# Scaling a transformer block's mixing products by 1/rms after they are made, with filler matmuls ahead of two norms

## What is computed

```
# end of the first block
x = x + gate2 * rmsnorm(y, g_post_ffn)
# second block, mixing input
h = rms_norm(x, norm_mix_w)          # x * rsqrt(mean(x*x) + eps) * w
proj = h @ w_in                      # 2048 x 5136
q_a, k_a, v_a, q_g, k_g, v_g, r_g, gate_lr = split_cols(proj, IN_SPLITS)
```

## Time and profile before

| | |
|---|---|
| median of 3 runs | 2810.79 us (2810.56 to 2812.27) |
| the profiled execution's own time | 2811.32 us |
| its span, first to last instruction | 2809.6 us |
| PE busy | 2719.9 us (97% of the span) |
| DVE busy | 1805.5 us (64%) |
| ACT busy | 1295.8 us (46%) |
| GpSimd busy | 292.1 us (10%) |
| mean granted clock of PE | 0.986 |

### The profile page before, as it was taken

The page is one execution under the profiler, slowest core; times in us unless marked ns, Lnnn a source line. Parts: engine busy times, 40 slices in busy tenths (PEclk is TensorE's granted clock), DMA queues, the critical chain, the costliest instruction groups (busy, mean ns, idle before and its releaser), DMA issues.

```text
span 2809.6 us, 38901 instructions
## 1 busy us (share of the span) xinstructions
PE 2719.9 (97%) x14799; PEld 2340.4 (83%) x14799; DVE 1805.5 (64%) x2009; ACT 1295.8 (46%) x1556; POOL 292.1 (10%) x161
## 2 busy tenths in 40 slices
PE   4899999999899999999997999999999999999998
PEld 4798888788688888888886989878888888888887
DVE  7966779689965556655576444656666654666655
ACT  2256554334444444444444445535555533555454
POOL 2010121100000100001000000100113210131100
PEclk8899999999999999999998999999999999999999
DMA  9975646698945557755576554545555565555553
GB/s 373 349 261 191 223 150 225 226 325 310 322 140 190 193 198 251 254 180 191 182 254 229 166 171 144 165 139 180 186 189 179 179 209 183 192 180 190 184 197 133
DMA packets 299522, 588.70 MB, mean 210 GB/s; under 512 B 12282, under 2 KB 19438, under 8 KB 298510
## 3 DMA queue, kind: packets, MB, share of 16 engines
q1 hardware_dynamic: 292816, 577.84, 60.5%
q10 hardware_dynamic: 6590, 9.27, 1.0%
HBM read 584.98 MB, written 2.10 MB: 209 GB/s over the span
## 4 chain that ended last, share of the span: by engine, by line
PE 88%; DVE 7%; issue 2%; ACT 1%; DMA 1%; SPq 0%; POOL 0%; DVEq 0%; POOLq 0%; ACTq 0%
PE psum L780 13%; PE psum L784 13%; PE psum L782 13%; PE bank L973 12%; PE psum L973 12%; PE bank L976 6%; PE psum L976 6%; PE psum L791 2%; PE psum L795 2%; PE psum L793 2%; DVE ada_acc L864 2%; DVE mod_acc L651 2%; DVE w_lo L738 2%; PE bank L946 1%; PE bank L2594 1%
## 5 line engine op out<-in xcount | busy, mean ns | idle before, releaser
L738 DVE TENSOR_TENSOR w_lo<-raw,w_hi 128x1024 fp32r<-128x1024 f32 x912 | 1157.0, 1286 | 835.9 <-ACT w_hi L726 826.0
L726 ACT ACTIVATE w_hi<-raw 128x1024 fp32r<-128x1024 f32 x912 | 953.1, 1054 | 1260.9 <-PE psum L784 580.7
L973 PE MATMUL psum<-h_both,w_hi 128*128 128x512 f32 x1408 | 496.5, 397 | 0.8 <-DVE x L2362 0.7
L973 PE MATMUL bank<-h_both,w_hi 128*128 128x512 f32 x1408 | 495.3, 396 | 0.0
L976 PE MATMUL bank<-h_both,w_lo 128*128 128x256 f32 x1408 | 395.0, 281 | 0.0
L976 PE MATMUL psum<-h_both,w_lo 128*128 128x256 f32 x1408 | 394.9, 280 | 0.0
L780 PE MATMUL psum<-w_hi,h_both 128*128 128x512 f32 x880 | 348.4, 396 | 1.3 <-ACT tokbuf L1810 0.7
L784 PE MATMUL psum<-w_hi,h_both 128*128 128x512 f32 x880 | 343.5, 390 | 0.0
L782 PE MATMUL psum<-w_lo,h_both 128*128 128x512 f32 x880 | 343.4, 390 | 0.0
L973 PEld LDWEIGHTS psum<-h_both,w_hi 128*128 128x128 f32 x1408 | 264.2, 188 | 64.1 <-DVE x L2362 1.0
L973 PEld LDWEIGHTS bank<-h_both,w_hi 128*128 128x128 f32 x1408 | 264.1, 188 | 63.3
(11 more groups left out here) (361 smaller groups left out, 3172.8 us busy)
## 6 DMA issues: line engine op xcount, KB each, us to landing
raw<-in_w_in_dram SPq DMA_DIRECT2D x120, 1024.0 KB, 5.1
raw<-in_w_ffn_in_dram SPq DMA_DIRECT2D x88, 1024.0 KB, 5.0
raw<-in_w_ffn_up_dram SPq DMA_DIRECT2D x88, 1024.0 KB, 5.1
raw<-in_w_ada_dram SPq DMA_DIRECT2D x64, 1024.0 KB, 5.2
raw<-in_w_ffn_out_dram SPq DMA_DIRECT2D x44, 1024.0 KB, 5.1
raw<-in_w_ffn_down_dram SPq DMA_DIRECT2D x44, 1024.0 KB, 5.1
ada_raw<-in_w_ada_dram SPq DMA_DIRECT2D x64, 512.0 KB, 8.0
raw<-in_w_out_dram SPq DMA_DIRECT2D x32, 1024.0 KB, 5.2
```

The lines of the kernel that those rows point to most:

```text
L726: nc.scalar.activation(w_hi[:, slot, :, 0:ncol], raw[:, rs, 2 * h:2 * h + 2, 0:ncol], ACT.Copy).then_inc(split_hi, inc)
L738: nc.vector.tensor_tensor(w_lo[:, slot, :, 0:ncol], raw[:, rs, 2 * h:2 * h + 2, 0:ncol], w_hi[:, slot, :, 0:ncol].bitcast(F32), ALU.subtra ...
L973: pe.matmul(region[:, f, :].rearrange("p (s t) -> p s t", s=2), w_hi[:, slot, kk, cols_], h_both[:, :, k, :], start=first, stop=False, ski ...
```

## The change

At norm2 PE transposes x itself, by a transpose with `ident`, as soon as a column block of the residual sum is there, without 1/rms. The products of all groups are therefore made of x times the gain, and 1/rms is applied where a group is taken out of PSUM. For that, DVE takes groups 0 to 3, 6 and 7 out (they need a factor that varies along the free axis, from `r_row`, made by two fp32 matmuls of `ones` by `diag` and a copy), and ACT takes 4, 5 and 9 to 12 out, each in two activations with a scale for each partition. The low-rank gate input moves from ACT to DVE. The order of residual pieces, squares, pairs and weight splits is written out anew on DVE, ACT and PE. ACT issues its four small loads after the norm. `keep_busy` puts 44 matmuls that nobody reads ahead of norm1 and 20 ahead of norm2. In `up2`, ACT and DVE each split one half of the second group's weights before, and not after, their work on the convolution of the first.

```diff
+        ("norm2", (2, 2, 2, 2)), ("r_row", (1, 0, 0, 0))]
...
+        def keep_busy(pe, stage, n):
+
+            pe.wait_ge(bank_free[0], fill(stage, 0))
+            for k in range(n):
+                pe.matmul(bank[:, 0, :].rearrange("p (s t) -> p s t", s=2), h_hi[:, k % KD, 0:P],
+                          h_both[:, :, k % KD, :], start=True, stop=True, skip_group_check=True)
...
# ACT
-            residual_squares_act(act, 3)
+            for c in range(D // COLS):
+                residual_square_act(act, 3, c, 0)
+                for b in (2 * c, 2 * c + 1):
+                    if b > 4:
+                        split_w_hi(act, plan.mix_in2, 0, b - 1, b)
+                    gained_pair_act(act, "norm2", b, gain_of("norm_mix_w_2"))
+                residual_square_act(act, 3, c, 1)
+            split_w_hi(act, plan.mix_in2, 0, 7, 8)
...
-            split_act(act, "norm2", h_hi, KD, gain_of("norm_mix_w_2"), between=plan.mix_in2)
...
-                    if g <= 12 and s == 2:
+                    if g in (4, 5, 9, 10, 11, 12) and s == 2:
...
+                        for t in range(TT):
+                            ins = nc.scalar.activation(dst[:, t, :], ps[:, t, :], kind,
+                                                       scale=stats[:, 4, 2 + t:3 + t])
+                        ins.then_inc(free, 1)
...
# ACT, up2
+                        if g == 0:
+                            split_w_hi(act, ph, i, *span(ph, 1, part=(0, 1)))
...
-                            split_w_hi(act, ph, i, *span(ph, 1, part=(0, 2)))
+                            split_w_hi(act, ph, i, *span(ph, 1, part=(1, 2)))
...
# DVE
             part_sums_dve(dve, 3, part_sq[:, 0])
-            split_w_lo(dve, plan.mix_in2, 0, 3, 4)
             dve.wait_ge(sem("y_gated"), 4)
-            residual_dve(dve, chain, 3)
-            normed_dve(dve, 4)
-            split_dve(dve, "norm2", h_hi, h_lo, KD, gain_of("norm_mix_w_2"), between=plan.mix_in2)
+            dve.wait_ge(sem("rms"), 4)
+            residual_columns_dve(dve, 3, 0)
+            residual_columns_dve(dve, 3, 1)
+            for b in range(KD // 2):
+                if b >= 4:
+                    split_w_lo(dve, plan.mix_in2, 0, b - 1, b)
+                gained_pair_dve(dve, "norm2", b, gain_of("norm_mix_w_2"))
+                if b < 2:
+                    residual_columns_dve(dve, 3, 2 + b)
+            split_w_lo(dve, plan.mix_in2, 0, 7, 8)
+            part_sums_dve(dve, 4, part_sq[:, 1])
...
+                    if at == (0, 0):
+                        split_w_lo(dve, ph, 0, *span(ph, 0, part=(4, 6)))
+                        normed_dve(dve, 4)
+                        split_w_lo(dve, ph, 0, *span(ph, 0, part=(6, 8)))
...
+                    if at == (0, 2):
+                        dve.wait_ge(bank_full[0], filled("r_row", 0))
+                        nc.vector.tensor_copy(r_row[:], bank[:, 0, 0:TOK]).then_inc(bank_free[0], 1)
+                        dve.wait_ge(bank_free[0], emptied("r_row", 0))
...
+                    if g in (0, 1, 2, 3, 6, 7) and s == 2:
+                        dve.wait_ge(w_used, ph.done(0, g))
+                        flat = psum[ph.pair[g]][:].rearrange("p b (f t) -> p (b f) t", t=TOK)
+                        per_token = r_row[:].unsqueeze(1).to_broadcast([P, 4, TOK])
+                        if g < 2:
+                            ins = nc.vector.scalar_tensor_tensor(q2_t[:, 4 * g:4 * g + 4, :], flat, HD ** -0.5,
+                                                                 per_token, ALU.mult, ALU.mult)
+                        else:
+                            dst = k2_t[:, 4 * (g - 2):4 * (g - 1), :] if g < 4 else (qg if g == 6 else kg)[:]
+                            ins = nc.vector.tensor_tensor(dst, flat, per_token, ALU.mult)
...
# PE
+            keep_busy(pe, "norm1", 44)
             pe.wait_ge(sem("normed"), 4)
...
+            ph = plan.mix_in2
+            keep_busy(pe, "norm2", 20)
+            for b in range(4):
+                pe.wait_ge(sem("x_ready"), 8 + 2 * (b // 2 + 1))
+                transpose_pair_pe(pe, "norm2", x, b)
+            for h in range(KD // 2):
+                products(pe, ph, 0, 0, h_hi, h_lo, transposed=True, ready="norm2", part=(h, h + 1))
+                if h < 4:
+                    pe.wait_ge(sem("x_ready"), 8 + 2 * (h // 2 + 3))
+                    transpose_pair_pe(pe, "norm2", x, 4 + h)
             pe.wait_ge(sem("normed"), 6)
-            normed_products(pe, ph, "norm2", 4, transposed=True)
+            pe.wait_ge(bank_free[0], fill("r_row", 0))
+            for t in range(TT):
+                mm = pe.matmul(bank[:, 0, t * P:(t + 1) * P], ones[:], diag[:, t, :], start=t == 0,
+                               stop=t == TT - 1, skip_group_check=True)
+            mm.then_inc(bank_full[0], 1)
```

More of the change, by code:

```diff
@@ L345, in bank_uses @@
         ("up1_1", (FFN_PARTS[1][1],) * 4), ("mod_down1", (0, 0, 0, 2)),
-        ("norm2", (2, 2, 2, 2))]
+        ("norm2", (2, 2, 2, 2)), ("r_row", (1, 0, 0, 0))]
     for at in sorted(SIDE_2):
@@ L419, in build_program @@
         diag = sb("diag", [P, TT, P])
+        r_row = sb("r_row", [P, TOK])
         trig = sb("trig", [P, 2, TT, ROT_HALF])
@@ L1740, in _ @@
                     split_w_hi(act, ph, 0, *span(ph, g, part=part if g else ((4, 8), (8, 8), (8, 8))[s]))
+                    if at == (1, 0):
+                        act.wait_ge(sem("rms"), 5)
+                        act.dma_start(w_up_g[:], a["w_gla_gate_up_2"][0]).then_inc(sem("w_up_g_full"), 16)
                     if at == (10, 0):
@@ L1759, in _ @@
                         nc.scalar.activation(lr_hi[:], raw_lr[:], ACT.Copy).then_inc(sem("lr_hi"), 1)
-                    if at == (4, 1):
-                        act.wait_ge(bank_full[1], filled("low_rank", 1))
-                        nc.scalar.activation(gate_lr[:], bank[0:RANK, 1, 0:TOK], ACT.Copy).then_inc(bank_free[1], 1)
-                    if g <= 12 and s == 2:
+                    if g in (4, 5, 9, 10, 11, 12) and s == 2:
                         act.wait_ge(w_used, ph.done(0, g))
@@ L2326, in up2_dve @@
                     for g in range(2):
-                        split_w_lo(dve, ph, i, *span(ph, g, part=(begun, 8) if g == 0 else None))
+                        split_w_lo(dve, ph, i, *span(ph, g, part=(1 if g else begun, 8)))
                         dve.wait_ge(sem("conv_low"), 2 * (g0 + i) + g + 1)
@@ L2337, in up2_dve @@
                                 dve.sem_inc(bank_free[b], 1)
+                        if g == 0:
+                            split_w_lo(dve, ph, i, *span(ph, 1, part=(0, 1)))
                         dst = (act_g, act_u)[g]
```

48 lines of the change are left out of this document (25 added, 23 removed).

## The result

| | before | after |
|---|---|---|
| median of the runs on the same chip, us | 2811.53 (2810.56 to 2813.80, 4 runs) | 2791.00 (2787.14 to 2796.14, 4 runs) |
| ratio, 95% interval | | 0.9927 (0.9909 to 0.9945) |
| profiled execution: time, span, us | 2811.3, 2809.6 | 2796.14, 2794.4 |
| PE busy | 97% | 98% |
| norm2: last product's start to first transposes, to first product, us | 15.05, 21.05 | 7.10, 10.04 |

The change gains 20.5 us by these medians, where 12.7 was forecast, and its time lies 4.8 us under the range. The forecast's direction holds and its size doesn't. Why it varies is part of the answer.

The account below looks back on a forecast made before the run. PE, busy 97% of the span, was taken as the bound. Norm2's 13.0 less 0.6 for the clock plus 0.3 at norm1 gave 12.7 us off 2811.3, 2798.6; the median 0.5 lower, 2798.1 us; range 2795.8 to 2802.5.

Parts of the forecast that it names:

- the paragraph on up2: In up2, moving one split past the convolution on ACT and DVE: 0, bounded by 1.2 us either way.
- Norm2: At norm2, first products 11.9 us earlier, cheaper transposes 1.5, two fp32 matmuls cost 0.4: gain 13.0 us at full clock.
- the clock term: At norm2, a fall of PE's clock after the pause costs 0 to 1.7 us; 0.6 taken in the sum.
- Pairs 4 to 7: In norm2's group 0, plain transposes cost 0.42 us a pair in place of 0.81: 1.5 us gained.
- rivals 3 and 4: Rival 3, and rival 4: fillers at the norms go at 0.39 us each, not 0.23, ending late: 2804 us, chance 0.07.
- Rival 3: At norm2, 1/rms comes too late for group 0's end, PE waits for `diag`: 2799.5 to 2802.5 us, chance 0.10.
- The clock: At norm1, PE's clock holding through the shorter pause gains between 0 and 1.6 us; 0.3 taken in the sum.
- Rival 1: PE's clock holds at both norms: gain 14.6 us, 2796.2 us, chance 0.20.
- Evictions on DVE, small loads: Six evictions moved to DVE are hidden by the splits' lead, and later small loads still come in time: 0 each.
- rival 5: DVE's queue starves PE at the six moved evictions, 2.88 us each, 17.3 us in all: 2815.4 us, chance 0.03.

Follow-up runs that it names:

- after_again: The changed kernel, with no further edit, run once more on another chip: median 2791.88 us against 2807.82 before there, ratio 0.9943.
- no_up2: The changed kernel with up2's order of weight splits put back as before: median 2794.99 us against 2807.82 before there, ratio 0.9951.

## Why the prediction was wrong, and where it was right

- **The step that failed** is the paragraph on up2: "0, bounded by one split's 1.2 us either way", for which it said that cover was the lead of four halves and that PE has no wait on `w_lo` there. PE has no such wait, but the lead isn't four halves: behind the convolution it fell to 0.5 to 0.7 us in one half of each group, and once, in the fourth group, to 0.16, and there PE went over to the long pace. In the profile up2 gained 7.8 us, of which 3.6 are this change of pace (3 to 4 by the medians) and 4.2 the pace of the second part, whose cause is open. My bound was one split's time, once; the loss was 0.053 us a half (8 pairs), on some 147 halves.
- **Norm2**: 12.4 us with the clock term, measured 11.7. The first product came 10.04 us behind the last matmul's start and not 9.1. DVE's sum of squares began 4.30 us behind that matmul where before had 3.89, and the clock fell, for which the sum had 0.6 and the runs show 0.5 to 1.0. Pairs 4 to 7 cost 0.36 each (0.42 taken), the fillers 0.23 apart, `diag` had a margin of 2.8 us (1.8 taken): rivals 3 and 4 are out. Rival 3's times were also added up wrongly: 1 to 3 us over 2798.1 are 2799.1 to 2801.1, and not 2799.5 to 2802.5, so the range reached 1.4 us too high, which made no difference here.
- **The clock**: 0.3 at norm1 as a mean is low. It is 1.3 to 2.6 us where it holds and about 0 where it doesn't, and it held in 9 of 14 profiles; the draw behind the first profile was one where it fell at both. Rival 1, that it holds at both, came true in some executions (after_again) and not in others. By the rule cited in the prediction (the Trainium skill, TensorE: Matmul & The Clock Gate, HAM oscillation) both pauses were short enough in all profiles with these fillers; the trace differs, since it fell behind a pause of 2.6 us at norm1 and around one of 2.2 us at norm2.
- **Evictions on DVE, small loads**: 0, as forecast. Nothing starved (rival 5), and one PSUM wait of 0.5 us went.
- **What the range left out**: the first profile of before had the long pace in up2 from its fourth group on and the short one in up1's first part. Up2's paces can give up to 7.8 us and those of up1's first part can take 4.8; the range, 6.7 us wide, had room for neither.
- **Sum with the missing term**: no_up2 gained 12.8 against 12.7. With up2's 7.8 the sum is 20.5, the first comparison's gain; with 3 to 4 it is after_again's 15.9. That is arithmetic and no proof: the other executions behind these medians have no profile, and in the profiled one up1 lost 4.8 us.

## What to carry to other kernels

Where one engine is busy for 97% of the span, read the mean distance from start to start in each stretch too, before and after, and not only its waits: here two stretches with the same matmuls, the same clock and no wait differ by 1.9%. When an edit moves work in a queue that feeds the bound engine, list the *leads* (end of the producer to start of its user), and treat one under 0.2 us as exposed, even with no wait beside it: 0.15 to 0.17 us changed the pace in three profiles of three, and 0.27 us in none of the places that had it. And judge an edit of a few us by several profiles: the changed kernel's first profile was 5.1 us above its own median, for up1's pace and the clock, which differ from execution to execution.

## What the runs showed of the hardware that I had not expected

- Alternating matmuls of 512 and 256 columns have two steady paces at the full granted clock, 0.3467 and 0.3533 us a pair. A stretch keeps the one that it started in, over hundreds of pairs, and, with no matmul added to each turn, changed it only at a split with a lead of 0.17 us or less. Four of one kind and then four of the other had one pace, 0.3505, in the one profile taken.
- Of 17 profiles with the alternating order and no matmul in each turn, up1's first part went at the long pace in 4, its second in 15, the two exceptions being those with two small matmuls ahead of it. With the new order of splits and nothing added to it, none of 13 profiles changed pace in up2's first part, and 2 had the long pace in its second.
- The granted clock fell around norm2's transposes in 7 of 14 profiles with the same 20 matmuls ahead of a pause of 1.7 to 2.6 us, and held in the other 7.
